# HGRN2 recurrent stage: decays as products of gates, directions in turn, narrow levels as 32x32 blocks

## What is computed

```
f = lb + (1 - lb) * sigmoid(z);  k = 1 - f;  q = silu(hq)
S_t = diag(f_t) S_{t-1} + k_t^T v_t;   o_t = q_t S_t
# direction 1 runs over the reversed tokens; the latent scan starts
# from the final context state of the same direction
decay = exp(b_t - b_s), b = cumsum(log f)          # within a chunk
A = einsum('td,sd,tsd->ts', q, k, decay)
o = A @ v + (q * exp(b)) @ S
```

## Time and profile before

| | |
|---|---|
| median of 3 runs (lowest to highest) | 3441.47 us (3430.22 to 3447.2) |
| span of the profiled execution | 3439.0 us; only its span is given |
| PE / PEld busy | 2775.5 us (81%) / 2306.7 us (67%) |
| DVE / ACT / POOL busy | 2075.3 (60%) / 1222.6 (36%) / 803.0 (23%) |
| mean granted TensorE clock | 0.892 of full speed |
| DMA | 848.12 MB moved, mean 247 GB/s |

### The profile page before, as it was taken

One profiled execution on the slowest core, in us unless ns is written; L12 is line 12 of the kernel. 1 busy time (PEld: TensorE's weight loads), 2 busy tenths in 40 slices (PEclk: granted clock), 3 DMA queues, 4 the chain that ended last, 5 costly groups with the idle time before them and its releaser, 6 DMA issues. The chain is left out here.

```text
span 3439.0 us, 38992 instructions
## 1 busy us (share of the span) xinstructions
PE 2775.5 (81%) x14561; PEld 2306.7 (67%) x14561; DVE 2075.3 (60%) x3720; ACT 1222.6 (36%) x2191; POOL 803.0 (23%) x724
## 2 busy tenths in 40 slices
PE   6999888995565565565666679989999999899998
PEld 5887677785455555455555667667888777778886
DVE  3224686587776854784455545357875465678753
ACT  2112433245555555555556531242220102422201
POOL 0002453124444444444444412001000000110000
PEclk9999999997777777767777879989999999999999
DMA  6999999789999999999999952202232231022222
GB/s 219 316 296 283 302 302 300 222 302 389 421 421 421 420 422 421 420 416 421 419 420 418 421 227 92 74 1 86 97 98 92 80 116 56 1 92 97 93 91 80
DMA packets 155057, 848.12 MB, mean 247 GB/s; under 512 B 15440, under 2 KB 15696, under 8 KB 88208
## 3 DMA queue, kind: packets, MB, share of 16 engines
q0 software_dynamic: 82624, 575.97, 41.5%
q1 hardware_dynamic: 72272, 269.99, 24.8%
HBM read 841.70 MB, written 136.31 MB: 284 GB/s over the span
## 5 line engine op out<-in xcount | busy, mean ns | idle before, releaser
L210 PE MATMUL PS<-AR_r,RHI 128*128 128x512 f32 (+2 forms) x1912 | 751.4, 393 | 27.4 <-DVE RING_r L1615 8.5
L909 PE MATMUL PS<-IDN,HL 128*128 128x128 f32 x2688 | 488.5, 353 | 331.0 <-ACT HL L1435 331.0
L212 PE MATMUL PS<-AR_r,RING_r 128*128 128x512 f32 (+2 forms) x1912 | 746.9, 391 | 0.0
L1821 DVE SCALAR_TENSOR_TENSOR AR<-AR 128x1024 f32<-128x1024 f32 x410 | 501.3, 1224 | 368.4 <-DMA AR<-peer_uv,XC 368.0
L909 PEld LDWEIGHTS PS<-IDN,HL 128*128 128x128 f32 x2688 | 423.0, 184 | 395.4 <-ACT HL L1435 388.4
L211 PE MATMUL PS<-AR_r,RHI 128*128 128x512 f32 (+1 forms) x1688 | 657.6, 390 | 0.0
L555 POOL DMA_INDIRECT AR<-peer_uv,XC x410 | 467.6, 1141 | 616.1 <-ACT HL L1435 315.1
L1613 DVE CAST RHI<-RING 128x1024 fp32r<-128x1024 f32 x256 | 178.7, 698 | 450.7 <-DMA RING<-in_wstream 448.1
L210 PEld LDWEIGHTS PS<-AR_r,RHI 128*128 128x128 f32 x1912 | 364.5, 191 | 107.7 <-issue 19.1
L212 PEld LDWEIGHTS PS<-AR_r,RING_r 128*128 128x128 f32 x1912 | 364.0, 190 | 74.1
L909 PE MATMUL PS<-IDN,AR 128*128 128x128 f32 x1408 | 255.4, 353 | 174.1 <-ACT AR L1435 174.1
(11 more groups left out here) (369 smaller groups left out, 3740.5 us busy)
## 6 DMA issues: line engine op xcount, KB each, us to landing
RING<-in_wstream SPq DMA_DIRECT2D x304, 512.0 KB, 3.5
peer_uv<-in_peer_u SPq DMA_DIRECT2D x50, 1024.0 KB, 17.1
peer_uv<-in_peer_v SPq DMA_DIRECT2D x50, 1024.0 KB, 17.7
peer_uv<-in_peer_u POOLq DMA_DIRECT2D x14, 1024.0 KB, 22.1
peer_uv<-in_peer_v POOLq DMA_DIRECT2D x14, 1024.0 KB, 23.0
AR<-peer_uv,XC POOLq DMA_INDIRECT x410, 14.5
XL<-in_xl SPq DMA_DIRECT2D x1, 2048.0 KB, 8.1
AR<-in_strips POOLq DMA_DIRECT2D x1, 2048.0 KB, 8.1
```

Source lines behind the costliest of these rows:

```text
L210: pe.matmul(out, sh, mh, start=start, stop=False)
L212: return pe.matmul(out, sl, mh, start=False, stop=stop)
L909: mm = pe.matmul(sum_bank(tt, k), scaled_row(n)[:, P * k:P * k + P], IDN[:], start=(j == 0 and k % 4 == 0), stop=(j == SLOTS - 1), is_tran ...
L1821: dve.scalar_tensor_tensor(u, u, 1.0, HT[:, n // SLOTS, :], ALU.mult, ALU.mult, accum_out=RAW[:, n:n + 1]).then_inc(dotted, 1)
```

## The change

Decays are no longer made from logarithms. The keys `KS[d]` (1 - f, over `EW` and the first half of `HL`), the queries `QE[d]` (q f) and the gates `Z[d]` grow in place: after level lv has been multiplied by TensorE, `grow_state` multiplies one half of each group's queries and keys by the total decay of the other half, and the total of the group is the product of its halves' totals, kept in one column of `Z[d]`. After the last level the totals are `EB` and the keys have their decay to the block's end. Clamp, logarithm, scan, exponentials and the subtractions go. POOL grows the context's columns, VectorE the latent ones.

The directions go in turn by level, with banks 2d and 2d + 1 each. In levels 0 to 5 only the four 32x32 blocks on the diagonal of each u are multiplied (64 small matmuls), into one bank, and taken under a mask of 32 columns into a compact `NEAR[d]`, which ScalarE copies into `AT` once. Level 6 multiplies two 32x32 blocks of each u, level 7 one of 64x64. `modulate` takes chunks in pairs: four first, two behind each level and direction up to level 5. There is one barrier (5) at the end, no `keep_clock` in the stage. SP's program is as it was. Lines of the changed kernel: small products L844, modulation L707, turned keys L864, updates L873, products of the outputs L883, growth L1757 and L1758, totals L1762, take L1770, copies L1380, L1387, L1394, L1401, states L1795, L1799.

```diff
@@ helpers
+        def grow(d, lv, cols):
+
+            m, half = 1 << (lv - 1), (1 << lv) - 1
+            q, k, f = (x[:, cols if x is not QE[d] else slice(0, 2048)].rearrange("p (n x) -> p n x", x=2 * m)
+                       for x in (QE[d], KS[d], Z[d]))
+            n = (cols.stop - cols.start) // (2 * m)
+            lo, hi = slice(0, m), slice(m, 2 * m)
+            of_lo, of_hi = f[:, :, m - 1:m], f[:, :, half:half + 1]
+            over_lo, over_hi = (x.to_broadcast([P, n, m]) for x in (of_lo, of_hi))
+            if d == 0:
+                return q[:, :, hi], over_lo, k[:, :, lo], over_hi, of_hi, of_lo
+            return q[:, :, lo], over_hi, k[:, :, hi], over_lo, of_hi, of_lo
...
-        B = HLF[:, 0:3072]
+        KS, NEAR = [EW, HLF[:, 0:3072]], [ar(8192, 512), ar(8704, 512)]
+        LEVELS, NEAR_LEVELS = 8, 6
@@ POOL
-                    pool.tensor_tensor(ev[:, :, qs], bv[:, :, qs], ref, ALU.subtract)
-                    pool.tensor_tensor(ev[:, :, ks], ref, bv[:, :, ks], ALU.subtract).then_inc(s["d"], 1)
...
+                for lv in range(1, LEVELS):
+                    steps.wait()
+                    _, _, ks, k_by, total, by = grow(d, lv, slice(2048, 3072))
+                    steps.done(pool.tensor_tensor(ks, ks, k_by, ALU.mult))
+                    steps.wait()
+                    ins = pool.tensor_tensor(total, total, by, ALU.mult)
...
+                ins.then_inc(hg["context"], 1)
@@ TensorE
             def modulate(n):
-                for _ in range(n):
+                for _ in range(n // 2):
                     i = next(made)
-                    modulation(FIRST["mod2"], [i], 6 + i // 16)
+                    modulation(FIRST["mod2"], (i, next(made)), 6 + i // 16)
+
+            def level(lv, d):
...
+                if lv >= 2:
+                    pe.wait_ge(hg["grown"], 2 * (lv - 2) + d + 1)
+                if 2 <= lv < LEVELS - 1:
+                    pe.wait_ge(hg["near"], 2 * (lv - 2) + d + 1)
+                if lv == LEVELS - 1 and d == 1:
+                    pe.wait_ge(hg["block"], 5)
+                q = QE[d] if lv else HQ
+                if lv < NEAR_LEVELS:
+                    blocks = [(32 * g, 32 * g, 32) for g in range(4)]
+                else:
+                    m = 1 << (lv - 1)
+                    blocks = [(a, a + m, m) if d == 0 else (a + m, a, m) for a in range(0, P, 2 * m)]
+                for u in range(16):
+                    for a, b, m in blocks:
...
+                        mm = pe.matmul(to[a:a + m, :], KS[d][:, P * u + a:P * u + a + m], q[:, P * u + b:P * u + b + m],
+                                       start=True, stop=True, skip_group_check=True)
+                mm.then_inc(hg["a"], 1)
+
+            modulate(4)
+            for lv in range(LEVELS):
+                for d in range(2):
+                    level(lv, d)
+                    if lv < LEVELS - 2:
+                        modulate(2)
...
+                for n, b in enumerate(HG_BLOCKS):
+                    if n >= 2:
+                        pe.wait_ge(hg["kz"], 6 * d + n - 1)
...
+                        mm = pe.transpose(bank(2 * d + n % 2, P * j, P), KS[d][:, a:a + P], IDN[:])
+                    mm.then_inc(hg["kt"], 1)
+            for d in range(2):
+                pe.wait_ge(hg["kz"], 6 * d + 6)
                 for j in range(5):
+                    if j >= 2:
+                        pe.wait_ge(hg["state"], 5 * d + j - 1)
@@ ScalarE
-                    act.activation(EW, Z[0], ACT.Ln).then_inc(s["lf"], 1)
...
-                    act.activation(e, e, ACT.Exp).then_inc(s["e"], 1)
...
+                act.activation(KS[d], Z[d], ACT.Identity, scale=-1.0, bias=par("one")).then_inc(hg["k"], 1)
@@ VectorE
-            for d in range(2):
-                dve.tensor_scalar(Z[d], Z[d], LN_MIN, None, ALU.max)
...
-                    dve.tensor_tensor_scan(turn(B[:, P * u:P * u + P]), ONES[:], turn(EW[:, P * u:P * u + P]), 0.0,
-                                           ALU.mult, ALU.add)
...
+                qs, q_by, ks, k_by, total, by = grow(d, lv, slice(0, 2048))
+                dve.wait_ge(hg["a"], 2 * lv + d + 1)
+                steps.wait()
+                dve.tensor_tensor(qs, qs, q_by, ALU.mult)
+                dve.tensor_tensor(ks, ks, k_by, ALU.mult).then_inc(hg["grown"], 1)
+                if lv < NEAR_LEVELS:
+                    take(d, lv)
+                dve.wait_ge(hg["grown"], 2 * (lv - 1) + d + 1)
+                steps.done(dve.tensor_tensor(total, total, by, ALU.mult))
...
+                    dve.wait_ge(hg["state"], 5 * d + j + 1)
```

More of the change, by code:

```diff
@@ L379, in build @@
         lb_ready = sem("lower_bound_ready")
[L380 to L383, removed]
+        hg = {k: sem(f"hg_{k}") for k in ("zero", "k", "q", "a", "grown", "near", "block", "context", "totals", "kt", "kz",
+                                          "u", "state")}
         ho = {k: sem(f"ho_{k}") for k in ("o", "sq", "sum", "root")}
@@ L503, in _ @@
             for d in range(2):
[L504 to L516, removed]
[L517 to L527 removed]
+                pool.memset(NEAR[d], 0.0).then_inc(hg["zero"], 1)
+            for d in range(2):
+                pool.memset(AT[d], 0.0).then_inc(hg["zero"], 1)
+            for d in range(2):
+                pool.wait_ge(hg["k"], d + 1)
+                for lv in range(1, LEVELS):
[4 more added lines that the diff above has]
+                    ins = pool.tensor_tensor(total, total, by, ALU.mult)
+                    if lv < LEVELS - 1:
+                        steps.done(ins)
+                ins.then_inc(hg["context"], 1)
+            passing(pool, 4)
+            barrier(pool, 5)
             for _ in range(4):
@@ L1389, in _ @@
+            for d in range(2):
+                act.wait_ge(hg["totals"], d + 1)
+                for n, b in enumerate(HG_BLOCKS):
+                    act.wait_ge(hg["kt"], 6 * d + n + 1)
+                    act.activation(Z[d][:, 512 * b:512 * b + 512], bank(2 * d + n % 2), ACT.Copy).then_inc(hg["kz"], 1)
+            passing(act, 4)
+            barrier(act, 5)
             for h in range(HG_HEADS):
@@ new lines, in take, with totals @@
+            def take(d, lv):
+                if lv >= 1:
+                    dve.wait_ge(hg["near"], 2 * (lv - 1) + d + 1)
+                mask = near[:, d, lv].unsqueeze(1).to_broadcast([P, 16, 32])
+                to, src = (x.rearrange("p (u t) -> p u t", u=16) for x in (NEAR[d], bank(2 * d + lv % 2)))
+                dve.copy_predicated(to, mask, src).then_inc(hg["near"], 1)
+            def totals(d):
+                dve.wait_ge(hg["context"], d + 1)
+                steps.wait()
+                dve.tensor_copy(EB[d].unsqueeze(2), Z[d].rearrange("p (u s) -> p u s", u=24)[:, :, P - 1:P]
+                                ).then_inc(hg["totals"], 1)
@@ L1774, in _ @@
+            for lv in range(LEVELS):
+                for d in range(2):
+                    if lv == 0:
+                        dve.wait_ge(hg["zero"], d + 1)
+                        dve.wait_ge(hg["a"], d + 1)
+                        take(d, lv)
+                    else:
+                        grow_state(d, lv)
+                    if lv == LEVELS - 1:
+                        totals(d)
+            for d in range(2):
+                dve.wait_ge(hg["totals"], 2)
                 for j in range(5):
-                    after(dve, s, "u", j + 1, 5)
```

173 lines of the change are left out of this document (61 added, 112 removed).

## The result

The changed kernel takes 3447.71 us (median of 20 runs, 3434.63 to 3458.78), the kernel before 3440.62 on the same chip: ratio **1.0022**, 95% interval 1.0013 to 1.0031. It is 7 us slower, within the 0.5% called the same; the forecast was 3452.

A forecast was written before the change was run, and what follows sets the result against it. DMA was taken to bound the recurrent stage; its end comes 12.7 us later through the longer tail, less 2.1 from paired chunks, net +10.6 on 3441.5: 3452 us, range 3424 to 3480.

The forecast's parts named there:

- DMA paces the loop: Levels 0 to 5: each step waits for two chunks, 11.7 us of DMA, against 9.7 us of TensorE work.
- first rival: Recurrent stage: DMA does not hold chunks back, engines set the pace; 3425 us, or 3355 with 15 ns instructions; 15 in 100.
- The tail: Work behind the stage's last chunk: pair, levels 6 and 7, transposes and states sum to 37.3 us, against 14.3 before.
- 61 ns a small product: Levels 0 to 6: cost of one 32x32 product instruction, from the row nearest in shape; 7.8 us a level.
- lower bound of 15 ns: Small products: lowest estimate per instruction, 61/4, as the moving operand is 32 wide instead of 128; 1.9 us a level.
- slow-product rival: Loop of levels: TensorE binds from 77 ns an instruction; at 121 ns the kernel takes 3531 us; 6 in 100.
- clock rival: Behind the last chunk: TensorE idling lowers its clock, doubled products and transposes add up to 28 us, 3480; 12 in 100.
- 2.1 less on TensorE's path to the output sums: After the stage: modulate(4) in pairs takes 2 x 1.94 us instead of 5.96.
- Carried to the end: After the stage: the net shift of +10.6 us passes through projection, wq and gathers to the kernel's end.

The follow-up runs named there:

- e1: The changed kernel with the 40 copies of 1 MB that follow chunks mod2 and mod3 issued behind chunk wq+3 instead: 3527.09 us, stage 102.4 us.
- e8: The changed kernel with sixteen 128x512 filler products ahead of each pair of chunks in the loop of levels: 3448.03 us.
- e7: The changed kernel with every 32x32 product of levels 0 to 5 issued twice: 3473.68 us.
- e11: The changed kernel with the last four modulation chunks, behind the outputs, multiplied one by one instead of in pairs: 3459.57 us in one run.
- e6: The changed kernel with pairs spread over the whole stage, the last two among the output products, and GpSimd's four copies behind barrier 6: 3425.99 us, ratio 0.9963.
- e5: The changed kernel with GpSimd's four 1 MB copies issued behind barrier 6 instead of behind barrier 5: 3444.19 us, ratio 1.0022 to the kernel before.

## Why the prediction was right

The mechanism was right and nearly all of its terms held. The number alone says little, since the range of 3424 to 3480 also holds the time of the kernel before; what carries the account is the stage, which e1 and the terms below test.

- *DMA paces the loop.* Forecast 11.7 us a pair, measured 11.4; chunk 27's pair starts at 531.1, forecast 533.5. e1 shows that it was DMA and not the engines. The first rival (3425 or 3355) is out: a chunk overtakes nothing.
- *The tail.* Forecast 37.3, measured 36.7: the pair 3.1 (1.9 forecast; it ran at a granted clock of 0.50, 1.2 GHz, as the chunk at 406.59 did), level 6 6.5 (7.8), level 7 6.6 (6.9), transposes 7.9 (7.8), states 12.6 (12.9). Stage end 567.8, forecast 570.8.
- *61 ns a small product* was nearly the right sum out of a wrong picture, and that is luck. Running, the products of levels 0 to 5 follow each other every 12 ns at full clock (the row at 391.15) and every 16 or 17 ns at a granted clock of 0.50 (103 in 1.70 us at 455.78); those of level 6 took 1.7 and 1.4 us for 64, 22 to 27 ns each. The lower bound of 15 ns was near the value. What made level 6 last 6.5 us is 3.1 us without instructions. The Trainium skill (TensorEngine Tiling (Array Packing), Instruction Overhead) gave an estimate of 3.2 us for level 6 at 2.4 GHz. The products themselves took 3.1, but most of them at a granted clock of 0.50 (534.0 to 536.8), where the same 60 cycles are an estimated 50 ns and 6.4 us: the trace is under the page's cost of one matmul here, as it is in levels 0 to 5. At full clock (e8) direction 0 of level 6 took 1.4 us, 22 ns a product.
- *The slow-product rival* (from 77 ns on) had its place right and its cause wrong. With twice the instructions a step binds from (11.7 - 1.9)/256 = 38 ns on; e7's average of 41 ns is just over that, its pairs came 13.8 us apart in the mean, and its stage grew by 33 us.
- *The clock rival* saw a granted clock of 0.62 to 0.70 in the loop, lower than I had thought likely, and 0.91 behind it. In the loop it cost nothing that can be measured (e8). In the tail it cost 1.2 us on the pair and 1.3 on direction 0 of level 7 (3.38 us at 540.76, against 2.05 for direction 1 at full clock): far from the 28 of the rival, since the clock was back for transposes and states.
- *The term that failed* is "2.1 less on TensorE's path to the output sums". The pairs were faster by 2.7 (3.29 against 5.96) and the outputs by 1.6, and all of it but 0.7 was lost at the third out chunk, cast 9.0 us later than before (592.28) behind a stage that ended 9.7 later. e11 took the 2.7 away again and the keys did not move against the stage's end. From the stage's end to the first gather the shift went from 9.7 to 8.6 us; forecast 12.7 - 2.1 = 10.6.
- *Carried to the end:* the last gather is 11.2 later, the medians differ by 7.1, forecast 10.6. From first to last gather the change takes 2.7 us longer than the kernel before, which is inside the spread of the table's kernels (1317.6 to 1322.3 us for that stretch). So it is luck that 11.2 is so near to 10.6; the shift that the stage passes on is 8.6.

## What to carry to other kernels

Where a queue is full through a stage, freeing the engines in it moves nothing; what counts is how much work is left behind the last transfer, and every transfer that the stage's end releases. Spread the uses of the stream over the stage's whole work, and then look at what the earlier end sets loose ahead of the stream: here neither alone could be told from nothing, and both together gave 0.4 to 0.6% against the kernel before. Products cut small to save arithmetic have a second price, their instructions; count these in the stage, not only their duration.

## What the hardware showed that I had not expected

- TensorE can run out of instructions. They come in packets of 16 KB, one for 256 instructions; 9 in the stage before, 18 now, 30 in e7. TensorE goes on 2.2 to 3.0 us after the packet's start, and it stood for up to 7.5 us (e6). The profile calls it "issue".
- 32x32 products that go to four different strips of 32 rows in turn follow each other every 12 ns at full clock (16 or 17 at a granted clock of 0.50), those that alternate between two strips every 22 (e8) and 27.
- The pace of a full DMA differs from execution to execution: 178.5, 179.7 and 184.7 us for the same stage in e5, the change and e11, with 321, 309 and 288 GB/s in 388.3 to 461.5 at shares of 1.02, 0.98 and 0.98.
